# Expert rows laid as (row, quarter) and moved two tiles a transfer, results sent with rows outermost, ring places given expert weights one by one

## The reference

```python
def routed_moe(h, router_w, router_b, w1, w3, w2):
    scores = jax.nn.sigmoid((h @ router_w).astype(F32))
    sel = (scores + router_b.astype(F32)).reshape(-1, N_EXPERT_GROUPS, EXPERTS_PER_GROUP)
    grp_score = jnp.sum(lax.top_k(sel, TOP_K)[0], axis=-1)
    best = jnp.argmax(grp_score, axis=-1)
    ...
    _, idx = lax.top_k(masked, TOP_K)          # 2 of 16 experts, both in the best of 4 groups
    gate = ...                                 # their scores, normalised to 1
    for e in range(N_EXPERTS):
        he = jax.nn.silu(h @ w1[e]) * (h @ w3[e])
        out = out + gate[:, e:e + 1] * (he @ w2[e])
    return out
```

## Time and profile before

| | us |
|---|---|
| median of 3 runs | 1935.04 |
| lowest, highest | 1932.84, 1939.7 |
| profiled execution, its own time | 1939.05 |
| span from first to last instruction | 1937.4 |
| PE busy | 1687.6 (87%) |
| DVE, ACT, POOL busy | 736.3, 370.4, 289.3 |

### The profile page before, as it was taken

The page is one execution under the profiler, slowest core; times in us unless marked ns, Lnnn a source line. Parts: engine busy times, 40 slices in busy tenths (PEclk is TensorE's granted clock), DMA queues, the critical chain, the costliest instruction groups (busy, mean ns, idle before and its releaser), DMA issues.

```text
span 1937.4 us, 22717 instructions
## 1 busy us (share of the span) xinstructions
PE 1687.6 (87%) x8794; PEld 894.7 (46%) x8795; DVE 736.3 (38%) x1303; ACT 370.4 (19%) x708; POOL 289.3 (15%) x284
## 2 busy tenths in 40 slices
PE   4988899899879879999999999999999829999690
PEld 0554455355355344544545555445565315554350
DVE  1144643753763464700017674213124232222124
ACT  2321232142132122000023333200010211111011
POOL 0003411431430440000000000000000032222114
PEclk9999899899889899999999999999989969999896
DMA  9611101021020015712110111113315369999973
GB/s 320 250 57 44 44 22 44 1 66 44 1 88 25 19 47 214 260 46 87 44 53 34 44 44 44 63 67 119 112 44 218 141 244 299 336 337 340 350 249 141
DMA packets 117777, 242.14 MB, mean 125 GB/s; under 512 B 17129, under 2 KB 26350, under 8 KB 117714
## 3 DMA queue, kind: packets, MB, share of 16 engines
q1 hardware_dynamic: 86800, 180.60, 27.1%
q0 software_dynamic: 22960, 49.17, 7.5%
q10 hardware_dynamic: 7954, 11.50, 1.7%
HBM read 219.10 MB, written 22.02 MB: 124 GB/s over the span
## 4 chain that ended last, share of the span: by engine, by line
PE 72%; DVE 13%; DMA 5%; ACT 3%; issue 3%; POOL 2%; ACTq 1%; SPq 1%; DVEq 0%; POOLq 0%; PEldq 0%
PE psum L425 15%; PE psum L437 8%; PE psum L999 7%; PE psum L715 6%; PE psum L602 4%; DMA arena<-exp_w_d 4%; PE psum L429 4%; PE psum L1021 3%; PE psum L830 3%; PE psum L660 2%; PE psum L628 2%; PE psum L499 2%; PE psum L447 2%; PE psum L864 1%; DVE arena L1662 1%
## 5 line engine op out<-in xcount | busy, mean ns | idle before, releaser
L425 PE MATMUL psum<-arena 128*128 128x512 f32 x688 | 311.4, 609 | 10.4 <-issue 4.6
L425 PEld LDWEIGHTS psum<-arena 128*128 128x128 f32 x688 | 131.8, 195 | 170.2 <-issue 162.4
L999 PE MATMUL psum<-arena 128*32 128x256 f32 x2816 | 170.2, 395 | 1.6 <-DVE arena L2007 1.5
L437 PE MATMUL psum<-arena 128*128 128x512 f32 x352 | 151.6, 592 | 0.0
L602 PE MATMUL psum<-arena 128*128 128x512 f32 x256 | 131.5, 644 | 1.2 <-ACT arena L1186 1.2
L999 PEld LDWEIGHTS psum<-arena 128*32 128x32 f32 x2816 | 93.9, 113 | 62.9 <-issue 11.6
L715 PE MATMUL psum<-arena 128*128 128x512 f32 x256 | 111.5, 593 | 0.0
L437 PEld LDWEIGHTS psum<-arena 128*128 128x128 f32 x352 | 66.8, 190 | 83.3 <-issue 83.2
L2069 POOL TENSOR_TENSOR arena<-arena 128x512 f32<-128x512 f32 x40 | 49.9, 1258 | 355.1 <-ACT arena L1241 305.7
L2105 POOL TENSOR_TENSOR arena<-arena 128x512 f32<-128x512 f32 x64 | 82.6, 1295 | 101.8 <-ACT arena L1281 101.8
L1618 DVE SCALAR_TENSOR_TENSOR arena<-arena 128x772 f32<-128x772 f32 (+1 forms) x96 | 93.9, 978 | 3.4
(11 more groups left out here) (344 smaller groups left out, 2119.3 us busy)
## 6 DMA issues: line engine op xcount, KB each, us to landing
arena<-exp_w_d SPq DMA_DIRECT2D x48, 2048.0 KB, 24.5
arena<-w_in_d SPq DMA_DIRECT2D x22, 2048.0 KB, 7.7
arena<-ada_w_d POOLq DMA_DIRECT2D x8, 2048.0 KB, 8.7
slots<-arena POOLq DMA_DIRECT2D x1, 9216.0 KB, 27.3
arena<-ada_w_d SPq DMA_DIRECT2D x4, 2048.0 KB, 23.1
arena<-ssd_proj_d SPq DMA_DIRECT2D x4, 2048.0 KB, 9.3
slots<-arena POOLq DMA_DIRECT2D x48, 128.0 KB, 6.6
arena<-slots POOLq DMA_DIRECT2D x46, 128.0 KB, 8.4
```

Source lines behind the costliest of these rows:

```text
L425: ins = mmul(ps[:, 0:T], slot[:, k, m * P:(m + 1) * P], src[:, k, C:NT], start=(k == 0), stop=(k == KD - 1))
L437: ins = mmul(ps[:, 0:n], src[:, k, t * P:(t + 1) * P], slot[:, k, 0:n], start=(k == 0), stop=(k == KD - 1))
L999: ins = mmul(psU[q * R:(q + 1) * R, 0:2 * HF], XT[:, k % 2, k // 2, :], w13[p][:, :, k, q * HF:(q + 1) * HF], start=(k == 0), stop=(k == K ...
```

## The change

Three things change.

1. **Layout and size of the transfers of x.** A tile now lies with partition = row * 4 + quarter, and one transfer loads both tiles of a batch. Its outermost size is 128 on both sides. DVE reads the turned x with the axes swapped accordingly (L2013 after the change), and writes XT as before. The results of PE, `psD`, keep the old layout, quarter * 32 + row.
2. **Sends.** The results of a batch go out in four transfers, one for each quarter, each with both tiles: 32 rows outermost, then the two tiles, then 256 columns, 64 KB. The counts of the semaphores `xrow_in` and `y_sent` follow (16 a load, 64 a batch of sends).
3. **First weights.** Expert 1's three transfers go into the ring places each when that place is over, the first ahead of the wait for the phase's end. Expert 2's exp_w2 follows expert 0's weights, its exp_w3 follows w_out's second half, and only its exp_w1 waits for `routeT`.

```diff
--- before.py
+++ after.py
@@ -1071,8 +1071,6 @@
                 if n == 0:
                     sp.dma_start(row, a["rows"]).then_inc(S_("rows_in"), 16)
 
-            sp.wait_ge(S_("phase_done"), ENG * 4)
-
             def weights(e, p, names):
                 for name in names:
                     src = a[name][0, e] if isinstance(e, int) else a[name][0, bass.ds(e, 1), :, :].rearrange("o r n -> (o r) n")
@@ -1082,13 +1080,23 @@
                         .then_inc(S_("w_in%d" % p), 16)
 
             UP, DOWN = ("exp_w1", "exp_w3"), ("exp_w2",)
+
+            def into_ring(n):
+
+                sp.wait_ge(*strip_over(n))
+                weights(1, 1, (UP + DOWN)[n % NS:n % NS + 1])
+
+            into_ring(len(strips) - 3)
+            sp.wait_ge(S_("phase_done"), ENG * 4)
+
             weights(0, 0, UP + DOWN)
-            for n in range(len(strips) - NS, len(strips)):
-                sp.wait_ge(*strip_over(n))
-            weights(1, 1, UP + DOWN)
-
+            weights(2, 2, DOWN)
+            into_ring(len(strips) - 2)
+            into_ring(len(strips) - 1)
+
+            weights(2, 2, UP[1:])
             sp.wait_ge(*is_full(("routeT",)))
-            weights(2, 2, UP + DOWN)
+            weights(2, 2, UP[:1])
             sp.wait_ge(S_("tiles_known"), 1)
 
             def renew(e, p):
@@ -1449,10 +1457,10 @@
 
             def x_row(j):
 
-                act.wait_ge(S_("xrow_in"), (j // BATCH) * (16 * BATCH) + 16 * BATCH)
+                act.wait_ge(S_("xrow_in"), (j // BATCH) * 16 + 16)
                 run(xq, xrow[:, bass.ds((j & (RING - 1)) * DQ, DQ)], ACT.Copy).then_inc(S_("xq_ready"), 1)
 
-            act.wait_ge(S_("xrow_in"), 16 * BATCH)
+            act.wait_ge(S_("xrow_in"), 16)
             run(xq, xrow[:, 0:DQ], ACT.Copy).then_inc(S_("xq_ready"), 1)
             act.wait_ge(S_("x_turned"), 1)
             run(xq, xrow[:, DQ:2 * DQ], ACT.Copy).then_inc(S_("xq_ready"), 1)
@@ -1469,7 +1477,7 @@
 
             gate(0)
             act.wait_ge(S_("x_turned"), 2)
-            act.wait_ge(S_("xrow_in"), 2 * 16 * BATCH)
+            act.wait_ge(S_("xrow_in"), 2 * 16)
             run(xq, xrow[:, 2 * DQ:3 * DQ], ACT.Copy).then_inc(S_("xq_ready"), 1)
             with act.Fori(1, n) as j:
                 hidden(j - 1)
@@ -2002,7 +2010,7 @@
             def modulate_x(n):
 
                 dve.wait_ge(S_("x_turned"), n)
-                v.tensor_tensor(XT, psX[:, 0:DQ].rearrange("p (i q r) -> p i q r", q=NQ, r=R), A2, ALU.mult).then_inc(S_("x_scaled"), 1)
+                v.tensor_tensor(XT, psX[:, 0:DQ].rearrange("p (i r q) -> p i q r", q=NQ, r=R), A2, ALU.mult).then_inc(S_("x_scaled"), 1)
                 dve.wait_ge(S_("x_scaled"), n)
                 v.tensor_tensor(XT, XT, B2, ALU.add).then_inc(S_("x_ready"), 1)
 
@@ -2014,7 +2022,7 @@
             def out_rows(done):
 
                 dve.wait_ge(S_("down_full"), done)
-                dve.wait_ge(S_("y_sent"), ((done + BATCH - 1) // BATCH) * (16 * BATCH))
+                dve.wait_ge(S_("y_sent"), ((done + BATCH - 1) // BATCH) * (16 * NQ))
                 v.tensor_tensor(ysb[:, bass.ds(((done + RING - 1) & (RING - 1)) * DQ, DQ)], psD[:, 0:DQ], g2q, ALU.mult)\
                     .then_inc(S_("y_ready"), 1)
 
@@ -2130,38 +2138,38 @@
                                             yo[:, t, :], None).then_inc(S_("x_sent"), 16)
             pool.wait_ge(S_("x_sent"), 16 * 2 * TL)
             pool.wait_ge(S_("x1_ss"), TL)
-            quarters = lambda tile: slots[bass.ds(tile * R, R), :].rearrange("r (q c) -> q r c", q=NQ)
-            part = lambda ring, tile: ring[:, bass.ds((tile & (RING - 1)) * DQ, DQ)]
+            half = lambda ring, b: ring[:, bass.ds((b & 1) * (BATCH * DQ), BATCH * DQ)]
+            rows = lambda b: slots[bass.ds(b * (BATCH * R), BATCH * R), :]
 
             def load_x(b):
-                for i in range(BATCH):
-                    pool.dma_start(part(xrow, b * BATCH + i), quarters(b * BATCH + i)).then_inc(S_("xrow_in"), 16)
+                pool.dma_start(half(xrow, b).rearrange("p (i c) -> p i c", c=DQ),
+                               rows(b).rearrange("(i r) (q c) -> (r q) i c", i=BATCH, c=DQ)).then_inc(S_("xrow_in"), 16)
 
             def send_y(b):
-                for i in range(BATCH):
-                    pool.dma_start(quarters(b * BATCH + i), part(ysb, b * BATCH + i)).then_inc(S_("y_sent"), 16)
+                for q in range(NQ):
+                    pool.dma_start(rows(b)[:, q * DQ:(q + 1) * DQ].rearrange("(i r) c -> r i c", i=BATCH),
+                                   half(ysb, b)[q * R:(q + 1) * R, :].rearrange("r (i c) -> r i c", c=DQ)).then_inc(S_("y_sent"), 16)
 
             load_x(0)
             pool.wait_ge(S_("y_ready"), 1)
-            for i in range(RING):
-                if i == BATCH:
-                    pool.wait_ge(S_("y_sent"), 16 * BATCH)
-                pool.dma_start(slots[(XTILES - 1 - i) * R:(XTILES - i) * R, :].rearrange("r (q c) -> q r c", q=NQ),
-                               ysb[:, i * DQ:(i + 1) * DQ]).then_inc(S_("y_sent"), 16)
-            pool.wait_ge(S_("xrow_in"), 16 * BATCH)
+            for i in range(2):
+                if i:
+                    pool.wait_ge(S_("y_sent"), 16 * NQ)
+                send_y(XTILES // BATCH - 2 + i)
+            pool.wait_ge(S_("xrow_in"), 16)
             load_x(1)
             n = pool.value_load(first_tile_i[0:1, NE:NE + 1], min_val=NE, max_val=XTILES - 3 * BATCH)
             nb = (n + (BATCH - 1)) // BATCH
             with pool.Fori(0, nb - 1) as b:
                 pool.wait_ge(S_("xq_ready"), b * BATCH + BATCH)
-                pool.wait_ge(S_("xrow_in"), b * (16 * BATCH) + 2 * 16 * BATCH)
+                pool.wait_ge(S_("xrow_in"), b * 16 + 2 * 16)
                 load_x(b + 2)
                 pool.wait_ge(S_("y_ready"), b * BATCH + BATCH + 1)
-                pool.wait_ge(S_("y_sent"), b * (16 * BATCH) + 2 * 16 * BATCH)
+                pool.wait_ge(S_("y_sent"), b * (16 * NQ) + 2 * 16 * NQ)
                 send_y(b)
             pool.wait_ge(S_("y_ready"), n + 1)
             send_y(nb - 1)
-            pool.wait_ge(S_("y_sent"), nb * (16 * BATCH) + 2 * 16 * BATCH)
+            pool.wait_ge(S_("y_sent"), nb * (16 * NQ) + 2 * 16 * NQ)
             pool.sem_inc(S_("pool_passed"), 1)
             for t in range(TL):
                 for i in range(2):
@@ -2173,7 +2181,7 @@
             for t in range(TL):
                 pool.wait_ge(S_("x2_ready"), t + 1)
                 g_.tensor_tensor(yo[:, t, :], xr[:, t, :], frow, ALU.mult).then_inc(S_("x2_rowed"), 1)
-            pool.wait_ge(S_("xrow_in"), nb * (16 * BATCH) + 16 * BATCH)
+            pool.wait_ge(S_("xrow_in"), nb * 16 + 16)
 
 
 # ---- launch ----
```

## The result

| | before | after |
|---|---|---|
| median, us (4 runs each) | 1935.36 | 1918.86 |
| lowest, highest | 1932.84, 1939.7 | 1917.43, 1919.8 |
| span of the profiled execution | 1937.4 | 1917.8 |

The ratio of the times is 0.9898, 95% interval 0.9871 to 0.9925: 1.0% faster, 16.5 us at the medians. The prediction was 1917 us. On other chips the same kernel gave 0.9916 (0.989 to 0.9941) and 0.9896 (0.9871 to 0.992).

The account below looks back on a forecast made before the run. Experts' weights landing late, slowed by loads of x, were taken to bound the kernel. Terms -17.1 -1.5 -0.5 +0.5 = -18.6 us gave 1920.4 on the profiled execution, 1916.4 from the median, said as 1917; range 1907 to 1938.

Parts of the forecast that it names:

- The bound and the loads: Experts' stage: weights landing late make PE wait 17.3 us; loads of x slow them, 300 GB/s a batch against 395.
- The steps of the recursion: Experts 10 to 15: landing of weights against PE's need, expert by expert; waits of 3.0 at 12 and 13, expert 15 at 1862.1.
- the places: Three places for experts' weights: expert e is ordered when e-3 is through; expert 10's is free only at 1747.8 us.
- the sends hardly do: Batches of the experts' stage: sends of y hardly slow the weights, 370 GB/s when they land against 223 with only loads.
- the term of -17.1: Experts' stage: x and y cost the weights 0.8 us a tile instead of 1.6, so expert 15 starts earlier, -17.1 us.
- Weights loaded earlier: Four of nine first transfers issued sooner: lead itself 0, clearing the scatter's way -1.5 us (bounds 0 and -2.0).
- POOL's issues: One load for two, four sends for two: 0 within the stage, -0.5 us at the start, +0.5 at the end.
- the end of the stage: Last sends: two more issues of 0.75 us on the chain, landing shrinks from 4.73; +0.5 us (-1 to +1.6).
- (1): Experts' stage: reading `slots` slows everything whichever engines do it, only the ends gain -1.5; 1933.5 us, chance 0.21.
- (2): Load behind four sends on POOL: x late, PE stops at L990 each batch; +20, 1955 us, chance 0.09.
- (3): Experts' stage: new sends slow weights as the loads do, 2.3 us a tile; +25, 1960 us, chance 0.05.
- (4): Experts' stage: the weights' rate improves by half only, -12 and -1.5; 1921.5 us, chance 0.20.

Follow-up runs that it names:

- halves: Kernel before with x in the new layout, a batch in two loads of 64 partitions, both tiles in each, 16 engines: ratio 0.9969.
- quarters: Kernel before with x in the old layout, a batch in four loads into 32 partitions each, both tiles in each, 16 engines: ratio 0.9969.
- all three loads that carry the gain: Against the kernel before, 128 partitions outermost: new load for both tiles 0.991, new layout one transfer a tile 0.9913, 1 KB of rows at 4 KB pitch 0.9915.
- whole rows with 4 outermost: Kernel before with x read in 4 pieces of 8 whole rows without gaps, on 4 engines, tiles getting other rows: ratio 1.0001.

## Why the prediction was right

**The bound and the loads: right.** The rate of the weights in the last hundred microseconds set the end, and the loads of x took it. Three things tell: with the new loads alone the 8 us of a batch went from 300 to 381 GB/s, the waits of L1010 from 17.3 to 7.2 us, and the stretch lost 13.5 us.

**The steps of the recursion: right within 2 us until expert 13, within 3.3 at expert 15.** It had weights of expert 12 land at 1805.1, a wait of 3.0; PE went on at 1804.11 after 4.26. Expert 13 1822.6 and 3.0; seen 1820.85 and 1.98. Expert 15 1862.1; seen 1858.80. Half of these 3.3 us was there at expert 13 (tile 3 started 1.6 us earlier than before the change); the other half is a first L999 at the low clock that the recursion put behind expert 13's wait, and that did not come: 3.66 us after a wait of 1.98. Before the change a wait of 1.95 us at expert 15 was followed by one of 5.35, so the length of the wait alone does not say which it will be. That the gain would be cut by the places shows at 1740 to 1750 us, with a DMA share of 0.33, and the first wait is at expert 12 as said. The term was -17.1 us; its two rows of the table give -19.0, and +0.6 before tile 3.

**The sends: missed.** I read the 370 GB/s at 1611 us as "the sends hardly do", kept that cost (4 us a batch at 370 instead of 395, 0.25 us) in the rate after the change, and so gave their new form nothing. They are worth 4.3 us in the stretch, alone and together, and the loads 13.5 where I had the whole 15.4 for them. The size fits the cost that I had kept: the 8 us after a load's issue have 381 GB/s with old sends and 394 with new, which is 0.27 us (one batch of each kernel). So the term of -17.1 was too small by 1.3 us against the -18.4 of the stage.

**The reason that I gave for the loads was half of it.** "4 of 16 engines" holds, but 16 engines do not cure it, as halves and quarters show. The other half of my ground, that the pattern becomes the one of the weights, is what all three loads that carry the gain have, and none of the others. It is a pattern that goes with the speed of loads; the new sends, 32 outermost, do without it.

**Weights loaded earlier: the lead 0, right; the scatter -1.5, wrong.** The weights are out of the scatter's way now, and it still takes as long (13.9 us from the first issue to the last landing, before and after). Its issues are 1.27 us apart for 0.52 MB, which asks for 412 GB/s, and from 1569 to 1577 us, with nothing else moving, the engines give 375 at a share of 0.95: it queues behind its own data. The landings of the earlier ones fell, as these lines of the scatters before and after (min, median, max us) show, but not that of the last, for which POOL waits:

```profile
DMA to landing us min/median/max: 4.7/4.8/4.9
```

```profile
DMA to landing us min/median/max: 3.4/4.2/4.7
```

**POOL's issues.** A load's issue takes 0.72 us, at the low end of my bounds. A send's takes 0.54, and lands in 1.9 to 6.1 us:

```profile
L2150 POOL DMA_DIRECT2D slots<-arena x96: 542/542/614, 1578.9 to 1878.0; - x96
...
DMA to landing us min/median/max: 1.9/4.9/6.1
```

So the end of the stage, where I had +0.5, came out at -1.4: the landing of the last send fell from 4.73 to 1.93 us on the chain of waits, more than two issues cost. The first load of all gave -1.2 for -0.5. Two of my zeroes held. DVE's strided read costs nothing (0.418 us, as before). DVE waits longer for sends (20.3 us in 16 times for 5.1 in 4), but none of it reaches PE: the one wait of 1.0 us that ends with DVE's L2026 is behind an L2026 that had itself waited for PE's L1021.

**The end of the program: not foreseen.** 2.5 us more come after ACT's last instruction, though the four transfers of the output land as before (2.6 to 4.8 us, median 4.0). It stands in every profile of a kernel with both new loads and new sends (10.21, 10.16, 10.20, 10.15) and in none of the others (7.69 to 7.78), those with one of the two included. The trace shows nothing in it, and its cause is open.

**The rivals.** (1) the rate stays: out, by the stretches of 2 us. (2) x late: out, from issue to ACT's copy it takes 6.4 us instead of 9.6. (3) sends as slow as loads: out, the reverse. (4) the rate improves by half only: out, since a batch's 8 us have 391 to 394 GB/s of the 395 without x and y. What holds the rest of the gain back is the places, as the recursion had it. The rule of the Trainium skill (DMA: Bandwidth & Descriptors, Rules for kernel authors) that transfers under 64 KB pay mostly overhead spoke against small sends, though these stay at its limit. The runs show that going from 128 to 64 KB with twice the count gained 4.3 us in the stretch, when it also spread them over all engines.

**How near the number is owes something to luck.** On the profiles I had -18.6 and -19.6 was found. Most terms missed by about as much or more: the stage by -1.3 us, the scatter by +1.5, the first load by -0.7, the last sends by -1.9, the end of the program by +2.5, and -1.0 lies ahead of the first scatter, whose start moves by more than that between kernels. They cancel. The main term, 17.1 of 18.6, stands on its own.

## What to carry to other kernels

When a stream of weights sets the end, look at the rate of the queue in stretches of 2 us, and see whose small transfers stand where it dips: here two loads of 0.13 MB cut 395 GB/s to 223 for everyone. Give a small load the partition pattern of the big one beside it, all 128 partitions outermost; 16 engines without that gave 2.8 and 7.7 of 13.5 us in one profile each. Find a stretch between two instructions that is free of what runs ahead of it: it told about 1 us apart where the ratios of the times have intervals of some 4 us to either side.

## What the runs showed of the hardware

**How many engines a transfer uses can be read off the packets.** A transfer that POOL issues with 4 outermost leaves 96 small packets more than one with 16 or more outermost, beside 32 of 4 KB. Before, 94 such transfers made 9024 of them. In the changed kernel they are gone: 17129 packets under 512 B became 8505, which is 17129 less 9024, plus 16 for each of the 25 transfers that it has more. POOL's queue has 8624 packets and 0.14 MB less, 16 bytes each. That the first kind runs on 4 engines is shown by the DMA share of 0.26 in the earlier trace rows. The same count fits every other kernel to within one packet: whole rows with 4 outermost (17129), new loads of one tile (46 times 96 fewer), halves (12714 for 12713), quarters (13449), the new sends alone (13289).

```profile
DMA packets 117776, 242.13 MB, mean 125 GB/s; under 512 B 17129, under 2 KB 26350, under 8 KB 117714
```

```profile
DMA packets 113360, 242.06 MB, mean 126 GB/s; under 512 B 12713, under 2 KB 21934, under 8 KB 113298
```

**More engines do not cure a small load by themselves.** Loads on 4 engines gave a stretch of 272.3 us, on 16 in two halves of the partitions 269.5, in four quarters 264.6, over all partitions 257.7. I had expected the halves to be nearer to the whole.
